# First loads in smaller parts, a slab rounded earlier, and a final norm split between ScalarE and VectorE in a two-layer hybrid block kernel

## The reference, cut to what matters

```python
def rms_norm(x, g):
    xf = x.astype(jnp.float32)
    y = xf * lax.rsqrt(jnp.mean(xf * xf, axis=-1, keepdims=True) + EPS)
    return (y * g.astype(jnp.float32)).astype(x.dtype)
...
    h = rms_norm(x, g_pre_mix)
    z = h @ w_in
...
    return x + gate[:, None, :] * (merged @ w_out)
...
    return rmsnorm(x, final_norm_w)
```

## Time and profile before

| what | value |
|---|---|
| time, median of 3 runs | 2528.84 us (2527.77 to 2528.96) |
| time of the profiled execution | 2526.38 us |
| span of the profiled execution | 2524.0 us |
| PE busy | 2489.1 us, 99% |
| ACT, DVE, POOL busy | 1075.1, 1154.5, 1140.6 us (43 to 46%) |
| DMA, mean over the span | 99 GB/s |
| granted TensorE clock, mean | 0.997 |

### The profile page before, as it was taken

How to read it: one execution, slowest core, us unless ns; L and a number is a source line. 1 busy time by engine, 2 the same in 40 slices (tenths; PEclk the granted TensorE clock), 3 DMA queues, 4 the chain that set the end, 5 groups by cost and what they waited for, 6 DMA issues and landing times.

```text
span 2524.0 us, 33037 instructions
## 1 busy us (share of the span) xinstructions
PE 2489.1 (99%) x13242; PEld 2141.8 (85%) x13242; DVE 1154.5 (46%) x2351; ACT 1075.1 (43%) x2062; POOL 1140.6 (45%) x672
## 2 busy tenths in 40 slices
PE   9999999999999999999999999999999999999998
PEld 8888888888888888889888888888898888898887
DVE  7681476755416772105233455522233345444313
ACT  7553498943335332225434333333344443333322
POOL 4354355544446454445343444534444434444442
PEclk9999999999999999999999999999999999999999
DMA  5233201145432553332322222222322222222232
GB/s 211 75 101 107 70 26 43 35 138 192 146 131 87 179 196 114 99 98 70 108 84 83 81 83 83 91 84 98 117 83 84 84 84 76 92 80 88 92 100 76
DMA packets 71768, 250.46 MB, mean 99 GB/s; under 512 B 7872, under 2 KB 12736, under 8 KB 71232
## 3 DMA queue, kind: packets, MB, share of 16 engines
q1 hardware_dynamic: 71616, 248.35, 29.4%
HBM read 246.22 MB, written 2.10 MB: 98 GB/s over the span
## 4 chain that ended last, share of the span: by engine, by line
PE 87%; ACT 6%; DVE 5%; POOL 1%; issue 1%; DMA 0%; SPq 0%; DVEq 0%; ACTq 0%; POOLq 0%
PE bank L1748 85%; PE bank L1758 2%; ACT PP L1966 1%; POOL w_lo L2823 1%; ACT pt_hi L1966 1%; ACT w_hi L1966 1%; ACT QQ L1966 1%; DVE pt_lo L2273 0%; DVE Y L2273 0%; DMA w_raw<-in_wa 0%; DVE XR L2273 0%; DVE C L2273 0%; DVE PP L2529 0%; DVE nt L2273 0%; ACT Hhi L1966 0%
## 5 line engine op out<-in xcount | busy, mean ns | idle before, releaser
L2823 POOL TENSOR_TENSOR w_lo<-w_raw,w_hi 128x1024 fp32r<-128x1024 f32 (+1 forms) x315 | 754.5, 2399 | 876.0 <-ACT w_hi L1966 875.8
L1748 PE MATMUL bank<-Hhi,w_hi 128*128 128x512 f32 (+1 forms) x1676 | 652.6, 389 | 0.0
L1748 PE MATMUL bank<-Hhi,w_lo 128*128 128x512 f32 (+1 forms) x1676 | 646.7, 386 | 0.0
L1748 PE MATMUL bank<-Hlo,w_hi 128*128 128x512 f32 (+1 forms) x1676 | 646.5, 386 | 0.0
L1966 ACT ACTIVATE w_hi<-w_raw 128x1024 fp32r<-128x1024 f32 (+1 forms) x319 | 326.1, 1026 | 121.4 <-DMA w_raw<-in_wa 80.9
L1748 PEld LDWEIGHTS bank<-Hhi,w_lo 128*128 128x128 f32 x1676 | 315.1, 188 | 64.7
L1748 PEld LDWEIGHTS bank<-Hlo,w_hi 128*128 128x128 f32 x1676 | 315.6, 188 | 57.7
L1748 PEld LDWEIGHTS bank<-Hhi,w_hi 128*128 128x128 f32 x1676 | 315.5, 188 | 57.5
L2823 POOL TENSOR_TENSOR w_fifth_lo<-w_fifth_raw,w_fifth_hi 128x1024 fp32r<-128x1024 f32 (+1 forms) x79 | 191.2, 2422 | 236.3 <-ACT w_fifth_hi L1966 236.3
L1748 PE MATMUL bank<-Hhi,w_fifth_hi 128*128 128x512 f32 x404 | 161.2, 399 | 0.0
L1748 PE MATMUL bank<-Hhi,w_fifth_lo 128*128 128x512 f32 x404 | 157.6, 390 | 0.0
(11 more groups left out here) (412 smaller groups left out, 4874.9 us busy)
## 6 DMA issues: line engine op xcount, KB each, us to landing
w_raw<-in_wb SPq DMA_DIRECT2D x169, 512.0 KB, 3.4
w_raw<-in_wa SPq DMA_DIRECT2D x139, 512.0 KB, 3.3
wm<-in_w_ada SPq DMA_DIRECT2D x48, 512.0 KB, 4.5
w_fifth_raw<-in_wb SPq DMA_DIRECT2D x42, 512.0 KB, 3.4
w_fifth_raw<-in_wa SPq DMA_DIRECT2D x35, 512.0 KB, 3.3
wa_raw<-in_wb SPq DMA_DIRECT2D x5, 512.0 KB, 5.4
XR<-in_x SPq DMA_DIRECT2D x4, 512.0 KB, 7.3
w1k<-in_w1k SPq DMA_DIRECT2D x1, 2048.0 KB, 8.3
```

Of the source, the lines that this page charges most:

```text
L1748: return self.e.matmul(o, lhs, rhs, start=start, stop=stop)
L2823: self.e.tensor_tensor(x.lo[:, k:k + n, :], x.raw[:, k:k + n, :], f(x.hi[:, k:k + n, :]), ALU.subtract).then_inc(*w_rest(s, k))
```

## The change

There are three parts. The first loads: `par` is now first, x part 0 is cut in two (k 0 and 1; k 2 and 3) and slab 0 in two (tiles 0 to 3; 4 to 7), issued alternately, and slab 0 is rounded after k = 1 and after k = 3. Slab 2 is rounded (`cut_to(2)`) ahead of `squares(1)` instead of behind it. The final norm: ACT multiplies x by the weight into `fin_all` as soon as a tile of x is finished (`weighted`), and DVE multiplies by the root in two instructions for each half, over five tiles (1280 elements a partition) and over three (768); the stores are cut the same way, 640 and 384 KB.

```diff
-    x_in = [lane(f"x_in{i}") for i in range(4)]
+    x_in = [lane(f"x_in{i}") for i in range(5)]
+    early_in = lane("early_in")
...
         def raw_input(self, h):
...
-                if h == 0 and k == 3:
-                    self.cut_to(0, 4)
+                if h == 0 and k in (1, 3):
+                    self.round_weights(0, self.slot[0], 2 * (k - 1), 4)
+                    self.rest_weights(0, self.slot[0], 2 * (k - 1), 4)
             if h == 0:
+                self.parts[0], self.cut = 4, 1
                 self.cut_to(1, 4)
...
             for n in self.norm_end(N, c, 4):
                 if h == 0:
+                    self.cut_to(2)
                     self.squares(1)
                     self.cut_to(3)
                 yield n
...
                 self.norm_add(N, n, XR[:, n, c], dve_proj.by("x", L, n, c.start), c)
+                if L:
+                    self.weighted(n, c)
                 return [dve_proj.by("x", L, n, c.start)]
...
-            for k in range(KT):
-                self.final(h, k, c, N, [N.m, x_ready[k, h], x_free])
-                if k % 4 == 3:
-                    self.store(h, k, c)
-            self.norm_read(N, dve_o.by("final", h, KT - 1))
+            for i, ks in enumerate(ENDS):
+                self.final(h, i, ks, c, N)
+                self.store(h, i, ks, c)
+            self.norm_read(N, dve_o.by("final", h, 1))
...
-            self.load_x(0)
             self.load_start()
-            self.send(1)
-            self.load_x(1)
+            self.load_x(0)
             self.send(1)
             self.load_x(2)
+            self.send(1)
             self.load_x(3)
+            self.load_x(4)
             self.load_masks(0)
             self.send()
...
+    X_PARTS = [(0, 0, 2), (0, 2, 4), (0, 4, 8), (1, 0, 4), (1, 4, 8)]
+    ENDS = [slice(0, 5), slice(5, 8)]
...
         def load_slab(self, s, x, dram, i, free):
+            if s == 0:
+                self.e.dma_start(x.raw[:, 0:4, :], dram[i][:, 0:4, :]).then_inc(*early_in(0))
+                self.load_x(1)
+                self.e.dma_start(x.raw[:, 4:8, :], dram[i][:, 4:8, :]).then_inc(*x.come(0))
+                return
...
         def round_weights(self, s, x, k, n):
-            self.wait_ge(x.come.by(s))
+            self.wait_ge(early_in.by(0) if (s, k) == (0, 0) else x.come.by(s))
...
+        def weighted(self, n, c):
+            self.wait_ge(dve_proj.by("x", 1, n, c.start))
+            self.put(fin_all[:, n, c], XR[:, n, c], ACT.Copy, scale=P("fin", n)).then_inc(
+                *act_o.named(*(("weighted", n, h) for h in range(2) if c in (ALL, HALF[h]))))
...
-        def final(self, h, k, c, N, points):
-            self.wait_ge(*points)
-            self.stt(fin_all[:, k, c], XR[:, k, c], P("fin", k), N.r, ALU.mult, ALU.mult).then_inc(*dve_o("final", h, k))
+        def final(self, h, i, ks, c, N):
+            self.wait_ge(N.m, act_o.by("weighted", ks.stop - 1, h))
+            x, n = fin_all[:, ks, c], ks.stop - ks.start
+            self.tt(x, x, N.r.unsqueeze(1).broadcast_to([128, n, 256]), ALU.mult).then_inc(*dve_o("final", h, i))
```

More of the change, by code:

```diff
@@ L408, in program @@
         rotate_first = rotate_second = rotate_split = ret_qk = ret_decay = ret_av = ret_stats = ret_aggr = ret_turn = nothing
-        att_split = ret_split = proj_gate = proj_att = proj_ret = x_out = final = nothing
+        att_split = ret_split = proj_gate = proj_att = proj_ret = x_out = weighted = final = nothing
         def stream(self):
@@ L661, in warm_up, with x_there @@
             self.freed[7] = [norm_sums.by("warm", self.n_warm)]
+        def x_there(self, h, k):
+            return x_in[[i for i, (h_, k0, k1) in enumerate(X_PARTS) if h_ == h and k0 <= k < k1][0]].by(0)
         def raw_input(self, h):
@@ L677, in squares @@
             for k in range(KT):
-                self.norm_add(self.first, k, XR[:, k, c], x_in[2 * h + k // 4].by(0), c)
+                self.norm_add(self.first, k, XR[:, k, c], self.x_there(h, k), c)
         def begin(self, h):
@@ L696, in begin @@
                 self.cut_to(5)
-            yield from self.normed(c, N, lambda k, c: x_in[2 * h + k // 4].by(0), ht[h], lambda k: P("g_pre_mix", k), None,
+            yield from self.normed(c, N, lambda k, c: self.x_there(h, k), ht[h], lambda k: P("g_pre_mix", k), None,
                                    None, par_in.by(0), odds=(2, 4, 6))
@@ L1318, in evac, with last @@
                 self.norm_add(N, n, XR[:, n, c], dve_proj.by("x", L, n, c.start), c)
+                if L:
+                    self.weighted(n, c)
                 return [dve_proj.by("x", L, n, c.start)]
             return evac
-        def last(self, h, N, x_ready, x_free):
+        def last(self, h, N):
             c = HALF[h]
@@ L1337, in walk @@
             self.stream()
+            self.load_start()
             self.load_x(0)
-            self.load_start()
-            self.send(1)
-            self.load_x(1)
             self.send(1)
             self.load_x(2)
+            self.send(1)
             self.load_x(3)
+            self.load_x(4)
             self.load_masks(0)
@@ L1638, in x_chain @@
                 if L:
-                    yield from self.last(h, N, x_ready, RS.spent)
+                    yield from self.last(h, N)
                     return
@@ L1683, in load_x @@
         def load_x(self, i):
-            c, ks = HALF[i // 2], slice(4 * (i % 2), 4 * (i % 2) + 4)
+            (h, k0, k1), c = X_PARTS[i], HALF[X_PARTS[i][0]]
+            ks = slice(k0, k1)
             self.e.dma_start(XR[:, ks, c], A["x"][:, ks, c]).then_inc(*x_in[i](0))
@@ L1732, in load_decay, with store @@
             self.e.dma_start(dec[r % 2][:, :], A["decay"][r]).then_inc(*decay_in[r % 2](L, r))
[L1734 to L1737, removed]
+        def store(self, h, i, ks, c):
+            self.wait_ge(dve_o.by("final", h, i))
+            self.e.dma_start(out[:, ks, c], fin_all[:, ks, c]).then_inc(*stored[h][i](0))
         def wait_stores(self):
@@ L1972, in round_weights @@
         def round_weights(self, s, x, k, n):
-            self.wait_ge(x.come.by(s))
+            self.wait_ge(early_in.by(0) if (s, k) == (0, 0) else x.come.by(s))
             self.put(x.hi[:, k:k + n, :], x.raw[:, k:k + n, :]).then_inc(*w_rounded(s, k))
         def gained(self, h, k):
-            self.wait_ge(x_in[2 * h + k // 4].by(0), par_in.by(0))
+            self.wait_ge(self.x_there(h, k), par_in.by(0))
             self.put(Ghi[k][:, HALF[h]], XR[:, k, HALF[h]], ACT.Copy, scale=P("g_pre_mix", k)).then_inc(*act_norm("raw", k, h))
```

## The result

| what | before | after |
|---|---|---|
| median | 2528.22 us (22 runs, 2525.80 to 2529.71) | 2531.82 us (22 runs, from 2530.33) |
| profiled execution | 2526.38 us | 2533.40 us |
| span of it | 2524.0 us | 2531.4 us |

The ratio is 1.0015, 95% interval [1.0009, 1.0021]: the change costs 3.6 us, 0.15%, which is under the 0.2% (5.1 us) that I took as tellable for one measurement; with 22 runs on each side the interval is clear of 1. (One of the 22 runs of after took 5476.19 us at a lower clock; the comparison leaves it out, and without it the highest is 2533.40.) The forecast was 2531.8.

A forecast was written before the change was run, and what follows sets the result against it. PE, busy 99% of the span, was taken to bound the kernel. Loads 0, slab 2 +3.2 and final norm -0.2 made +3.0 on 2526.38: 2529.4 for a like execution, 2531.8 as a median; range 2526.6 to 2534.0.

The forecast's parts named there:

- Slab 2 ahead of the squares: Half 1's squares: POOL's slab 2 work holds DVE's adds, PE resumes at 27.5 instead of 23.76; +3.2 us kept to the end.
- rival (a): Held once only: the sixth add gets in ahead of POOL, PE +1.7, total +0.8 us, 2529.6; chance 0.17.
- the clock behind the long wait: After PE resumes at 27.5: half clock to 32.0 costs 2.2 us against 1.6 before, +0.6.
- The upper bound of this term: Slab 2 step: at most 4.9 us, from 3.7 of wait plus another half-clock stretch, nothing given back.
- First loads: Kernel start: bytes set landings, x for k = 4 to 7 still at 8.64; 0 us, bounds 0.9 loss, 1.0 gain.
- Rival (c): Clock falls 3.4 us behind PE's thin first 24 matmuls, row sums and root 1.2 us late; total +4.2; chance 0.14.
- the root still near 17.4: Sign expected in the profile after: the first root does not move; a moved root would show the forecast wrong.
- (c) with late loads: Clock fall behind the thin first matmuls, plus loads late by 0.9 us: total +5.1 us, 2533.9.
- The final norm: Kernel end: two finals take 2.43 us for 3.22, the end moves with the first store; -0.2 us.
- the rival price for the wide instruction: DVE's finals at the end: each 256 takes 0.624 us, so the 1280-element final 3.12 against 1.69; first store +1.3.
- rival (b): It gains: x of k = 4 to 7 lands 1.0 sooner, DVE not held, half-clock stretch gone; -2.8 us, 2526.0; chance 0.12.
- (d): Nothing: the adds are not held and the loads change nothing; +0.1 - 0.2 us, 2528.7; chance 0.12.

The follow-up runs named there:

- e2: Kernel before with slab 2 rounded ahead of the squares and nothing else: 2531.27 us (11 runs), ratio 1.0014.
- e3: Kernel before with the change's new first loads and slab 0 roundings and nothing else: 2528.12 us (11 runs), ratio 1.0001.
- e4: Kernel before with the changed final norm, including its cut of the stores, and nothing else: 2526.79 us (11 runs), ratio 0.9994.
- e5: On e2, POOL begins slab 2's remainder only after DVE's last add of squares of half 1: 2528.96 us (11 runs), ratio 1.0003 to before.
- e1: Kernel after, with slab 2 rounded behind the squares again: 2528.10 us (11 runs), ratio 0.9999 to before.
- e6: Kernel before with the load of par issued ahead of x part 0 and nothing else: 2526.62 us, one run.
- e11: On e3, seven warm-up multiplications fill PE's pause between k = 3 and k = 4 of the first product: 2528.20 us (11 runs), ratio 1.0001 to before.
- e9: Kernel before with the changed final norm and the copy of the roots to RT moved ahead of slabs 2 and 3: 2526.31 us (11 runs), ratio 0.9996.
- e10: Kernel before with the copy of the roots to RT moved ahead of slabs 2 and 3, old final norm: 2526.93 us (11 runs), ratio 0.9998.
- e7: Kernel before with only slab 0 loaded in two halves, one behind the other: 2528.24 us, one run.
- e8: Kernel before with only x part 0 loaded in two parts, one behind the other: 2527.38 us, one run.
- e12: Kernel before with only the stores cut as in the change, the eight finals kept: 2528.03 us (10 runs), ratio 1.0002.

## Why the prediction was right, and where it was not

The number, 2531.8 against 2531.82, is closer than the steps deserve. The forecast put +3.0 on the median of three runs, 2528.84; over 22 runs before's median is 2528.22 and the difference 3.6. The two misses of 0.6 cancel, and that is luck. The parts alone don't add up to it closely either: +3.3 (e2), +0.1 (e3) and -1.2 (e4) make 2.2, which is no contradiction with such intervals, but no proof of each term.

**Slab 2 ahead of the squares** (forecast +3.2). Right in mechanism, and in size within the interval. Each add that meets a POOL instruction ends 0.28 to 0.29 us behind it, as read from the earlier trace rows; POOL gets in front of the sixth add, as forecast and against rival (a), which needed slab 3 to be rounded 0.2 us later. e2 has the forecast's own clock: PE at 27.30 for 27.5, chain 3.3 later for 3.2, and +3.3 in the median. The wait for `TR` goes, as said. e5 shows that the overlap is the cause. One term of it was mis-sized: the clock behind the long wait. I took +0.6. Counted over windows of half a microsecond from 6 to 40 us, before loses 1.71 us to the lower clock and e2 3.42: two stretches, from 26.3 on. About 0.5 us of that fell into PE's wait and cost nothing, so it is +1.2. With 3.5 for the wait (27.30 against 23.76) PE was 4.7 behind at 61 us, where the sum had 4.3; what `TR` had spare absorbed that. That a stretch follows the wait at all was no safe premise: e1, e3, e4 and e6 have the same wait of 1.02 and no stretch behind it. The upper bound of this term doesn't add up as written either: 3.7 and a whole further stretch (1.7 lost) are 5.4, not 4.9.

The Trainium skill (SBUF — State Buffer, Who interferes with whom and Summary: rules for kernel authors) says that VectorE with two SBUF inputs and a GpSimd instruction that reads SBUF exclude each other for the whole instruction, and that the one which starts first decides. This trace agrees for the first add (held from 21.29 to 23.41). It adds one thing: POOL, ready for slab 3 while DVE had its adds queued without a pause, got in between the fifth and the sixth.

**First loads** (forecast 0, bounds -1.0 to +0.9). This is the step that failed. "bytes set these landings and not the issue. x for k = 4 to 7 then lands at 8.64 again": the landing is at 9.74 in the profile of after and 0.9 to 1.1 late in all four profiles with these loads. The bytes ahead of it are the same, but two more loads stand in the train, this one is issued 0.90 later, and the rate in the meantime is lower: e3 moved 246 to 297 GB/s in each microsecond from 3 to 8, before 291 to 390. The bound I had named for the case that the issue counts, 0.9, was nearly its size. Why the landing is late stays open between the issue and the number of loads. The rule of 2 us for each load, which the prediction weighed (the Trainium skill, DMA: Bandwidth & Descriptors, anatomy of one DMA), would have made 4 us; the trace shows a quarter of that for two loads. That section is on transfers issued by GpSimd, and these are issued by SP.

**Rival (c)**, the clock behind the thin first product, was given 0.14, with the test "the granted clock between 11 and 15 is under 1". The test came out for it: 0.63 from 11.5 to 14 in after. "the root still near 17.4" was wrong by 2.0, 1.1 of landing and 0.9 of clock (e11), and a root that moves was one of the signs the prediction had named for being wrong: in its own terms the first loads were wrong, though the number came out. For (c) with late loads I had +5.1 in a like execution; the profile of after stands 5.5 behind before's from 111 us on. So in the profiled execution rival (c) is what happened, on top of the forecast's own mechanism.

Why the median is nevertheless the forecast's: the loads that put after's profile back by 2 us change the medians by nothing that can be told (e3 1.0001, e1 0.9999). Before's profile holds fewer slow stretches than its other runs are likely to have: its mean granted clock is 0.997, and that of before's 33 runs beside e1 to e4 is 0.9958. In the first 40 us the clock's loss comes in equal pieces: 0 in e4, e6, e9 and e10, 1.71 in before, e1, e3, e5, e7, e8, e11 and e12, 3.42 in e2, 5.12 in after. Of those with 1.71 and the old loads, before has it at 25, e5 and e12 at 17 to 18. And between 253 and 1510 us after falls from 5.5 to 7.4 us behind before, all of it at half-clock stretches near 322 and 820 us, where other kernels show fewer or more. As far as one profile for each kernel can say, a profile is thus a draw of these pieces, and the difference of two profiles (7.0) is that of the kernels (3.6) and of the draw. Whether the late landing costs its 1.7 us in a typical run or is given back in a stretch that then doesn't come, these runs don't settle. The clocks lean to the second: the mean over e3's 11 runs is 0.9965, above before's 0.9958, but each is on record to three places only.

**The final norm** (forecast -0.2). Right: -0.2 in e4's span, by the first store as said, and the rival price for the wide instruction (3.12 us) is out at 1.49. I had left the 2.38 us outside the span as they were; they are 2.02 in after and 2.03 in e4, 0.35 less, and I can't attribute it.

**A gain**, rival (b), needed x sooner and no hold; both failed. (d), nothing, is excluded by e2.

## What to carry to other kernels

Before you pull work of one engine ahead, look at what it releases: here 1 us of ScalarE work moved forward set free a GpSimd instruction that ran into VectorE's two-input additions, and the median rose by 3.3 us; with the GpSimd instruction made to wait it rose by 1.2, which can't be told from nothing. When the sum is a few microseconds, compare each part by medians and read a profile for its order and its waits, not for its total, since two profiles can differ by several half-clock pieces of 1.7 us (three ahead of the end in before, one in e9, seven in after), and the mean clock of one kernel's runs varies too (0.995 to 0.997 in before). And an earlier release gains only up to the next chain that sets the end: of 2.8 us won at 29 us, 1.0 was left at 69.

## What the hardware showed that I had not expected

- With two more loads ahead of it and the same bytes, a load landed 1.1 us later, and the rate on the way was lower (246 to 297 GB/s in e3 against 291 to 390). It was issued 0.90 later, though still 6.3 to 6.6 us ahead of its landing.
- With the loads unchanged, the same landing came at 8.36 to 8.64 us in seven of eight profiles, and at 9.58 in one.
- The lower clock came, ahead of the last 10 us, in stretches of 3.4 us, single or two in a row: 1.71, 3.42 and 5.12 us were lost between 6 and 40 us, nothing between. Filling PE's pause with multiplications kept the clock at 1.00 from 11.5 to 15.5, and the stretch came at 18.8 instead.
- Two VectorE instructions back to back can be parted by a waiting GpSimd instruction (at 25.41), and each held add ends 0.28 to 0.29 us behind the one that held it.
- The time outside the span is the same within 0.1 us for all runs of a kernel and differs between kernels, 1.80 (e9), 2.02 (after), 2.17 (e10) and 2.38 (before), without a visible cause.
